# A two-block network on one core: rows of a gate-up projection shared by two and three weight panels, one set of squares summed by GpSimd

## The reference, cut to what matters

```python
h = h + 0.5 * swiglu(rmsnorm(h, ffn1_norm), ffn1_w_gate, ffn1_w_up, ffn1_w_down)
...
x = x + rms_norm(out2, post_mix_norm)
h = rms_norm(x, pre_ffn_norm)          # x / sqrt(mean(x*x) + eps) * gain
... h @ w_up ...                       # 1024 x 5632, gate and up columns
```

## Time and profile before

| what | value |
|---|---|
| median of three runs | 2650.37 us |
| span of the profiled execution (its own time) | 2652.1 us |
| TensorE matmuls | 2500.1 us busy, 94% of the span |
| VectorE | 1343.2 us, 51% |
| ScalarE | 874.8 us, 33% |
| GpSimd | 120.6 us, 5% |
| share of TensorE in the chain that ended last | 89% |

### The profile page before, as it was taken

One profiled execution on the slowest core, in us unless ns is written; L12 is line 12 of the kernel. 1 busy time (PEld: TensorE's weight loads), 2 busy tenths in 40 slices (PEclk: granted clock), 3 DMA queues, 4 the chain that ended last, 5 costly groups with the idle time before them and its releaser, 6 DMA issues.

```text
span 2652.1 us, 32094 instructions
## 1 busy us (share of the span) xinstructions
PE 2500.1 (94%) x13027; PEld 1981.6 (75%) x13038; DVE 1343.2 (51%) x2030; ACT 874.8 (33%) x1457; POOL 120.6 (5%) x156
## 2 busy tenths in 40 slices
PE   8999999997989999999999997888996899999997
PEld 6888888874445888888888877677885688788886
DVE  5544344436673446554433763343364552877723
ACT  4222223322444223322222433433335232433321
POOL 0000000000232000000000000232000000000000
PEclk9999999897799999999999996988996789999998
DMA  5333343310000333333333330000130023233331
GB/s 161 96 96 93 103 112 108 87 52 0 1 1 16 96 96 115 88 96 96 97 98 92 95 83 14 2 1 2 47 90 24 18 78 96 65 96 96 96 98 54
DMA packets 366419, 189.04 MB, mean 71 GB/s; under 512 B 11329, under 2 KB 363841, under 8 KB 366273
## 3 DMA queue, kind: packets, MB, share of 16 engines
q1 hardware_dynamic: 366272, 187.00, 24.8%
HBM read 184.87 MB, written 2.10 MB: 71 GB/s over the span
## 4 chain that ended last, share of the span: by engine, by line
PE 89%; DVE 6%; ACT 3%; issue 1%; DMA 0%; POOL 0%; another core or an unknown queue 0%; DVEq 0%; SPq 0%; ACTq 0%; POOLq 0%
PE ps L407 24%; PE ps L409 24%; PE ps L408 24%; PE ps L655 2%; PE ps L926 1%; PE ps L674 1%; PE ps L893 1%; PE ps L1549 1%; PE ps L789 1%; PE ps L1333 1%; PE ps L1338 1%; PE ps L1343 1%; PE ps L519 1%; PE ps L477 1%; PE ps L335 1%
## 5 line engine op out<-in xcount | busy, mean ns | idle before, releaser
L407 PE MATMUL ps<-u_hi,w_hi 128*128 128x512 f32 x1968 | 779.1, 396 | 0.9 <-DVE qkv L1469 0.9
L408 PE MATMUL ps<-u_lo,w_hi 128*128 128x512 f32 x1968 | 769.5, 391 | 0.0
L409 PE MATMUL ps<-u_hi,w_lo 128*128 128x512 f32 x1968 | 769.4, 391 | 0.0
L362 DVE TENSOR_TENSOR w_lo<-w_raw,w_hi 128x1024 fp32r<-128x1024 f32 (+2 forms) x366 | 422.7, 1156 | 274.4 <-ACT w_hi L378 273.5
L378 ACT ACTIVATE w_hi<-w_raw 128x1024 fp32r<-128x1024 f32 (+2 forms) x366 | 365.6, 1000 | 446.2 <-PE ps L409 443.0
L407 PEld LDWEIGHTS ps<-u_hi,w_hi 128*128 128x128 f32 x1968 | 368.1, 187 | 88.0 <-issue 4.9
L408 PEld LDWEIGHTS ps<-u_lo,w_hi 128*128 128x128 f32 x1968 | 368.0, 187 | 85.7 <-issue 5.9
L409 PEld LDWEIGHTS ps<-u_hi,w_lo 128*128 128x128 f32 x1968 | 367.8, 187 | 81.7 <-issue 0.8
L409 PE MATMUL ps<-mid_hi,w_lo 128*128 128x512 f32 x528 | 208.6, 395 | 0.0
L407 PE MATMUL ps<-mid_hi,w_hi 128*128 128x512 f32 x528 | 208.6, 395 | 0.0
L408 PE MATMUL ps<-mid_lo,w_hi 128*128 128x512 f32 x528 | 208.5, 395 | 0.0
(11 more groups left out here) (373 smaller groups left out, 2889.8 us busy)
## 6 DMA issues: line engine op xcount, KB each, us to landing
w_raw<-w_in_dram SPq DMA_DIRECT2D x101, 512.0 KB, 3.8
w_raw<-ffn_w_gate_dram SPq DMA_DIRECT2D x44, 512.0 KB, 3.8
w_raw<-ffn_w_up_dram SPq DMA_DIRECT2D x44, 512.0 KB, 3.9
w_raw<-w_up_dram SPq DMA_DIRECT2D x44, 512.0 KB, 3.8
w_raw<-ffn_w_down_dram SPq DMA_DIRECT2D x32, 512.0 KB, 4.1
w_raw<-w_out_dram SPq DMA_DIRECT2D x24, 512.0 KB, 4.0
w_raw<-w_down_dram SPq DMA_DIRECT2D x16, 512.0 KB, 4.0
w_raw<-ffn_w_down_dram SPq DMA_DIRECT2D x16, 384.0 KB, 3.4
```

The source lines that it names most:

```text
L362: dve.tensor_tensor(lo, raw, hi.bitcast(F32), ALU.subtract).then_inc(w_split, 1)
L407: pe.matmul(out, wh, h_k, start=k0 + k == 0, stop=False)
L408: pe.matmul(out, wh, l_k, start=False, stop=False)
L409: mm = pe.matmul(out, wl, h_k, start=False, stop=end)
```

## The change

The first gate-up projection takes its first two panels together: for each row block k, the ones matmul, then three matmuls of panel 0, then three of panel 1. The loads and the ScalarE and VectorE work on panel 1 move from behind row block 3 to behind row block 1. The third gate-up projection takes its first three panels together. Its squares are added up in `acc` by GpSimd, and one ones matmul stands behind panel 0's last block, ahead of the last three matmuls of panels 1 and 2. The order of VectorE's work is as before.

```diff
+    def multiply_abreast(pe, name, hi, lo, wide, ready, after=None):
+        s = segs[name]
+        for k in range(DK):
+            for j in range(wide):
+                slot, out = (s.base + j) % RING, ps[(s.group + j) % BANKS][:, :]
+                if k == 0:
+                    pe.wait_ge(w_split, s.base + j + 1 + RING)
+                    pe.wait_ge(bank_read, s.group + j + 1)
+                if j == 0:
+                    ready(k)
+                wh, wl, end = w_hi[:, slot, k, :], w_lo[:, slot, k, :], k == DK - 1
+                pe.matmul(out, wh, hi[:, k, :], start=k == 0, stop=False)
+                pe.matmul(out, wh, lo[:, k, :], start=False, stop=False)
+                mm = pe.matmul(out, wl, hi[:, k, :], start=False, stop=end)
+                if end:
+                    mm.then_inc(w_used, 1)
+                    if after and j == 0:
+                        after()
...
-    ADDED, SUMMED, SPLIT = (1, 2, 3, 4, 5, 7), (0, 6), (0, 1, 2, 3, 4, 6)
+    ADDED, SUMMED, SPLIT = (1, 2, 3, 4, 5, 7), (0,), (0, 1, 2, 3, 4, 6)
...
+        elif q == 6:
+            if k >= 3:
+                act.wait_ge(row_added, k - 2)
...
+    def add_squares_pool(pool, q):
+        for k in range(1, DK):
+            pool.wait_ge(norm_sq, DK * q + k + 1)
+            if k > 1:
+                pool.wait_ge(row_added, k - 1)
+            pool.tensor_tensor(acc[:, :], acc[:, :], pair_a[:, k % 2, :], ALU.add).then_inc(row_added, 1)
...
     def norm_sum_pe(pe, q, size=SEQ):
-        pe.wait_ge(sq_added, (DK - 1) * (ADDED.index(q) + 1))
+        if q == 6:
+            pe.wait_ge(row_added, DK - 1)
+        else:
+            pe.wait_ge(sq_added, (DK - 1) * (ADDED.index(q) + 1))
...
-            for first, last, x in ((0, 1, range(0, 4)), (1, 2, range(4, 8)), (2, 3, ())):
+            for first, last, x in ((0, 1, range(0, 2)), (1, 2, range(2, 8)), (2, 3, ())):
...
-            multiply(pe, "ffn1_up", u_of(u_hi), u_of(u_lo), ready=summed_rows_pe(pe, 0))
+            multiply_abreast(pe, "ffn1_up", u_hi, u_lo, 2, summed_rows_pe(pe, 0))
+            multiply(pe, "ffn1_up", u_of(u_hi), u_of(u_lo), done=2)
...
-            multiply(pe, "ffn3_up", u_of(u_hi), u_of(u_lo), ready=summed_rows_pe(pe, 6))
+            multiply_abreast(pe, "ffn3_up", u_hi, u_lo, 3, split_rows_pe(pe, 6), after=lambda: norm_sum_pe(pe, 6))
+            multiply(pe, "ffn3_up", u_of(u_hi), u_of(u_lo), done=3)
...
             for k in range(DK):
                 act.wait_ge(x_in[k], 16)
                 upper_rows_act(act, 0, k, h, u_hi)
-                if k % 4 == 3:
+                if k in (1, 7):
                     upper_part(act, 1 + k // 4)
...
                 lower_rows_dve(dve, 0, k, h, u_hi, u_lo)
-                if k % 4 == 3:
+                if k in (1, 7):
                     lower_parts(dve, 2 + k // 4)
```

More of the change, by code:

```diff
@@ L386, in build, with multiply @@
     hi_done, cst_in, panels_asked = sem("hi_done"), sem("cst_in"), sem("panels_asked")
-    def multiply(pe, name, hi, lo, n=SEQ, ready=None, ready_group=0, after=None):
+    def multiply_abreast(pe, name, hi, lo, wide, ready, after=None):
[16 more added lines that the diff above has]
+                        after()
+    def multiply(pe, name, hi, lo, n=SEQ, ready=None, ready_group=0, after=None, done=0):
         s = segs[name]
@@ L394, in multiply @@
             for j in range(s.per):
+                if i == 0 and j < done:
+                    g += 1
+                    continue
                 slot = (s.base + j) % RING
@@ L425, in build @@
     NORM_GAIN = ("ffn1", "mix", "mem", "ffn2", "pre_mix", "post_mix", "pre_ffn", "post_ffn")
-    ADDED, SUMMED, SPLIT = (1, 2, 3, 4, 5, 7), (0, 6), (0, 1, 2, 3, 4, 6)
+    ADDED, SUMMED, SPLIT = (1, 2, 3, 4, 5, 7), (0,), (0, 1, 2, 3, 4, 6)
+    MEANS = (1, 2, 3, 4, 5, 6, 7)
+    row_added = sem("row_squares_added")
     def gain(q, k):
@@ L488, in norm_root_act @@
         else:
-            act.wait_ge(norm_mm, ADDED.index(q) + 1)
+            act.wait_ge(norm_mm, MEANS.index(q) + 1)
         act.activation((acc_m if q == 2 else acc)[:, :], ps[7][:, 0:size], ACT.Sqrt, bias=stat[:, 95:96], scale=1.0 / D).then_inc(norm_rt, 1)
@@ L1809, in _ @@
             gdn_pool(pool)
+            add_squares_pool(pool, 6)
         @blk.tensor
```

## The result

The changed kernel took 2656.45 us (median of 20 runs, 2653.39 to 2657.40), the kernel before 2651.30 (20 runs, 2649.52 to 2655.36). On the 2650.37 us of the first three runs, on which the forecast was built, it is +4.2 us (+2.7 to +6.1), 2654.6 us: inside the range of 2646.5 to 2656.0 and under 0.2%, but slower beyond its own interval, and by more than the +1.0 us forecast. The median as it stands, 2656.45, is 0.45 us above the upper end of that range.

A forecast was written before the change was run, and what follows sets the result against it. TensorE was taken to bound the kernel (89% of the chain). First projection 0, third projection -0.4 and clock +1.4 summed to +1.0 us, 2651.4 us, with a range of 2646.5 to 2656.0.

The forecast's parts named there:

- First projection, 0: First gate-up projection: TensorE has no gap to close and panels 1 and 3 arrive in time, so 0 us.
- TensorE alone: Third projection: by TensorE's own pace the ones matmul ends at 2280.4, the six left at 2281.8, 5.8 us ahead.
- What is late next: Third projection: panel 3's lower part ends 5.98 us behind the ones matmul; TensorE stands 4.6 us, 1.2 us gain left.
- The seven adds: Third projection: GpSimd's adds stretch VectorE by 0.7 us per row block; panel 3 starts at 2287.2, -0.4 us against before.
- costs TensorE little: Third projection: the claim that block 7's `u_lo`, ready at 2279.2, hardly delays TensorE.
- The sign that I had set for this: Third projection: TensorE idling over 2 us for `u_lo` inside the three panels would show the forecast's core wrong.
- The clock: Third projection: the 4.6 us stand before panel 3 lowers TensorE's clock; +1.4 us, bounds 0 and +2.0.
- rows 9's price: Earlier low-clock stretch of 4.4 us at 0.50: 10 matmuls, each 0.20 us dearer, +2.0 us.
- the prediction's own worst case: Panel 3 +3.8 us (adds stretching 1.4 us per block) plus the clock's full 2.0 us.
- The clock holding: Rival: the clock holds through the stand before panel 3; -0.4 to -1.2 us, 2649.6 us, chance 0.2.
- Strict turns at 1.4 us per block: Rival, third projection: GpSimd and VectorE alternate without overlap over six row blocks; +5.8 us, 2656.2 us, chance 0.13.
- The full gain: Rival, third projection: panel 3's lower part not behind the reciprocal, so 5.8 us stay; 2644.6 us, chance 0.04.

The follow-up runs named there:

- without adds: Changed kernel with GpSimd's seven adds of norm 6 left out, so only row block 0 is summed: 2653.96 us, ratio 1.0003 to the kernel before.
- one panel ahead: Changed kernel, each third-projection panel's parts made one panel sooner; norm 6 squares added by VectorE (ratio to before 0.9983) or, in a second version, GpSimd (0.9986).
- the one with VectorE's adds: Changed kernel with the squares of norm 6 added by VectorE instead of GpSimd, three panels still together: 2654.58 us, ratio 1.0005 to the kernel before.
- two abreast: Changed kernel with two panels taken together in the third projection instead of three: 2653.09 us, ratio 1.0000 to the kernel before.
- panel 3 early: Changed kernel with VectorE making panel 3's lower part ahead of the reciprocal in the third projection: 2652.48 us, ratio 1.0001 to the kernel before.

## Why the prediction was right or wrong

- **First projection, 0:** right. Alone it gave 1.0002, and TensorE was busy for 48.99 of 49.00 us. The small spare of panel 3 held.
- **TensorE alone:** right. The ones matmul was put at 2280.4, zero + 21.7; without adds it ended at 21.5.
- **What is late next, 5.98 us behind the ones matmul:** right. 2278.17 + 5.98 = 2284.15, and the lower part ended at 2282.92 + 1.22 = 2284.14. The stand of 4.6 us was forecast as 4.6.
- **The seven adds:** the stretch per row block was right (0.7 taken, 0.70 measured), what followed from it was not. The step that failed is that `u_lo` "costs TensorE little", with the last add as what the ones matmul waits for. For block 7, of which I had said it, it is true, and the last add came when it should: put at 2280.3, zero + 21.6, measured zero + 21.7 (2276.27). But TensorE came to it only at 2277.30, so that wait did not exist. With the adds VectorE's row block of 2.69 us is longer than TensorE's nine matmuls (9 x 0.23 = 2.1). In the timeline of PE blocks 3, 4, 5 and 6 start at 2266.54, 2268.91, 2271.93 and 2274.29, each 0.05 to 0.06 us behind the end of its `u_lo`, and with their slower first matmul they cost 0.4, 0.3, 0.95 and 0.3 us against TensorE's own pace. The largest is block 5, where the stretch of 1.03 us on blocks 1, 3 and 5 falls; TensorE stood 0.69 us there. The adds cost 2.1 us at the ones matmul (23.6 against 21.5), where I had charged 0.8; panel 3 started at +0.7 instead of -0.4 us. I had tested the cover at the last block alone, instead of at each. The sign that I had set for this, over 2 us of idle time for `u_lo` inside the three panels, was too coarse: the waits listed are 0.9 us.
- **The clock:** it fell, as forecast, but the term of +1.4 was mis-sized: 2.4 us, and 2.7 with the slower first matmul behind the stand, which I had put at nothing. I had taken two thirds of rows 9's price because the fall comes late in the stand; it stayed for 5.1 us after TensorE went on, longer than the 4.4 of rows 9. My upper bound of 2.0 was too low.
- **Sum:** +1.0 forecast; +0.7 + 2.7 + 0.3 = +3.7 in the profile, +4.2 (2.7 to 6.1) in the runs. That it stays under 0.2% held, and so did the range, but narrowly: the prediction's own worst case, 2650.37 + 3.8 + 2.0 = 2656.2, already lay 0.2 us above the upper end that was said to hold it. The forecast's +1.0 was a -0.4 and a +1.4; both came out over a us higher, and the sum misses by as much.
- **Rivals.** The clock holding: no; the rows here had one price and one stand of that length, and the runs show that the time of the fall varies (last section). Strict turns at 1.4 us per block: half of that. A meeting costs 1.03 or 0.37 us, and every second row block has the larger one, the next the smaller. The Trainium skill's rule (SBUF — State Buffer, Who interferes with whom) that the second of the two is stopped until the first is done agrees with the rows: the 1.77 us L480 ended 0.56 us behind the add. But the rule alone doesn't say how often the two meet; here three L480 grew by 1.03 us and three L1765 by 0.37 beside seven adds. The full gain: no, as argued; but the run one panel ahead shows that 5.1 us of it are there once panel 3 and those after it are made sooner.

## What to carry to other kernels

Letting several panels share a row block uses up the work behind the shared part. Before widening it, list what the next panel waits for, from the last shared instruction on, and compare it with what is left to cover it; then test the cover at every block and not at the last alone. When a stand appears, moving its cause forward by one place for all panels helped, while moving two and leaving the third moved the stand and made it longer. And an idle engine isn't free help: GpSimd's adds cost the busy VectorE as much as doing them itself, and a us more in the chain.

## What the runs showed of the hardware that was not expected

- A stand of 2.2 us left TensorE's clock at 2.4 GHz; one of 2.9 us and those of 4.6 us dropped it to 1.2 GHz (one profile each for the first two, four for the last). For the same stand of 4.6 us it came back 5.1 us after TensorE went on in the changed kernel, 3.7 us in the run without adds and 2.9 us in the one with VectorE's adds. Nor did it fall at the same place: in the changed kernel it was 1.00 for the first two us of the stand (2279.50 to 2281.50) and 0.50 from 2282.50 on, while in the run without adds it stayed at 1.00 through the whole stand (2281.40 to 2286.00) and read 0.54 in the 3.6 us after. So the length of a stand alone does not tell how much the fall costs. The rule behind this was not tried. The six waits of two abreast (8.1 us in all, 3.7 of them at the start, with the clock already low) did not drop it.
- The tail differs for the same reason. From the first matmul of the down projection to the end it is 141.6 us before, 141.9 in the changed kernel and 142.8 with panel 3 early. The small matmuls that spread the last norm took 1.16 us in the changed kernel and 2.08 in the one with panel 3 early, where the granted clock was 0.58 from 2635.00 to 2636.07 and 0.50 behind it; in the changed kernel it was 1.00 to 2637.40. The timelines of PE, changed kernel and panel 3 early:

```profile
2636.16 1.16 PE L558 MATMUL ps<-cst,stat 128*128 128x128 f32 x8 [0.57 <-DVE stat L1759]
```
```profile
2636.07 2.08 PE L558 MATMUL ps<-cst,stat 128*128 128x128 f32 x8 [0.57 <-DVE stat L1759]
```

- GpSimd's add of two full 128x512 operands takes 1.34 us with hardly any two-input instruction beside it, and 1.47 to 1.78 with one; VectorE's same add (L491 in the run one panel ahead) takes 0.68.
